# Three jobs taken from TensorE's transposes and fp32 products in a two-block hybrid layer

## The reference, cut to what matters

```python
# GDN (first layer): per head and chunk, from the log gates g
g_cum = cumsum(g); diff = g_cum[:, None] - g_cum[None, :]
decay = exp(where(incl, diff, 0)) * incl
# retention (second layer)
rq = rotary(rq.reshape(B, T, 8, 64), pos)
rk = rotary(rk.reshape(B, T, 8, 64), pos)
ret = chunk_retention(rq, rk, rv)         # products rk^T rq, weighted by distance
# cross attention (second layer): keys and values of the memory
kv = rmsnorm(mem, g_mem) @ w_xkv          # mem: (256, 1024)
```

## Time and profile before

| | us |
|---|---|
| median of 3 runs | 889.11 (888.86 to 889.22) |
| the profiled execution, its own time | 889.3 |
| its span | 887.5 |
| busy in the span: TensorE / VectorE / ScalarE / GpSimd | 879.3 / 594.3 / 440.9 / 167.7 |

### The profile page before, as it was taken

The page is one execution under the profiler, slowest core; times in us unless marked ns, Lnnn a source line. Parts: engine busy times, 40 slices in busy tenths (PEclk is TensorE's granted clock), DMA queues, the critical chain, the costliest instruction groups (busy, mean ns, idle before and its releaser), DMA issues.

```text
span 887.5 us, 12630 instructions
## 1 busy us (share of the span) xinstructions
PE 879.3 (99%) x4991; PEld 757.1 (85%) x4991; DVE 594.3 (67%) x868; ACT 440.9 (50%) x619; POOL 167.7 (19%) x181
## 2 busy tenths in 40 slices
PE   8999999999999999999999999999999999999998
PEld 6887887888988999988888889888888888889786
DVE  5478988996796666744456647977785576665542
ACT  6265456864545555533344436646555444443531
POOL 0432225765110000000000002100100024444700
PEclk9999999999999999999999999999999999999999
DMA  8874542344244666656577635523542567775762
GB/s 301 199 253 144 189 143 92 120 134 127 86 127 159 190 190 189 190 189 190 190 227 270 190 97 191 184 102 106 179 143 75 166 198 220 220 220 158 238 224 71
DMA packets 86627, 152.64 MB, mean 172 GB/s; under 512 B 10016, under 2 KB 18000, under 8 KB 86448
## 3 DMA queue, kind: packets, MB, share of 16 engines
q1 hardware_dynamic: 80352, 144.55, 50.8%
q0 software_dynamic: 3696, 3.76, 2.1%
q10 hardware_dynamic: 2528, 3.63, 1.1%
HBM read 147.59 MB, written 1.44 MB: 168 GB/s over the span
## 4 chain that ended last, share of the span: by engine, by line
PE 95%; DMA 3%; ACT 1%; POOL 1%; DVE 0%; issue 0%; SPq 0%
PE gemm L515 71%; PE gemm L1012 5%; PE mixbank L1012 5%; DMA raw<-in_w_in_dram 2%; PE mixbank L578 2%; PE mixbank L677 1%; PE mixbank L702 1%; DMA raw<-in_w_down_dram 1%; PE mixbank L782 1%; PE mixbank L873 1%; PE mixbank L1184 1%; PE gemm L1212 1%; PE mixbank L688 1%; PE mixbank L725 1%; POOL w_lo L2647 1%; PE mixbank L1101 0%
## 5 line engine op out<-in xcount | busy, mean ns | idle before, releaser
L1825 DVE TENSOR_TENSOR w_lo<-raw,w_hi 128x2048 fp32r<-128x2048 f32 (+3 forms) x131 | 285.3, 2187 | 181.5 <-ACT w_hi L1274 181.4
L1274 ACT ACTIVATE w_hi<-raw 128x2048 fp32r<-128x2048 f32 (+3 forms) x140 | 255.5, 1833 | 196.9 <-DMA raw<-in_w_in_dram 48.8
L515 PE MATMUL gemm<-w_hi,s_hi 128*128 128x512 f32 (+3 forms) x784 | 208.7, 386 | 0.5 <-ACT s_hi L1298 0.3
L515 PE MATMUL gemm<-w_lo,s_hi 128*128 128x512 f32 (+3 forms) x784 | 201.7, 377 | 0.1
L515 PE MATMUL gemm<-w_hi,s_lo 128*128 128x512 f32 (+3 forms) x784 | 201.7, 377 | 0.0
L515 PEld LDWEIGHTS gemm<-w_lo,s_hi 128*128 128x128 f32 x784 | 142.6, 188 | 27.7 <-DVE w_lo L1825 0.3
L515 PEld LDWEIGHTS gemm<-w_hi,s_lo 128*128 128x128 f32 x784 | 142.7, 188 | 27.6
L515 PEld LDWEIGHTS gemm<-w_hi,s_hi 128*128 128x128 f32 x784 | 139.8, 188 | 26.5 <-issue 2.5
L2653 POOL TENSOR_TENSOR sm<-sm 128x2 f32<-128x2 f32 (+5 forms) x13 | 21.6, 1662 | 453.1 <-DVE sm L1869 297.3
L2778 POOL DMA_DIRECT2D hid_moved<-hid_blocks x96 | 54.9, 580 | 70.0 <-DVE hid_blocks L2596 67.8
L2647 POOL TENSOR_TENSOR w_lo<-raw,w_hi 128x2048 fp32r<-128x2048 f32 x9 | 41.4, 4609 | 39.1 <-ACT w_hi L1274 39.1
(11 more groups left out here) (353 smaller groups left out, 1172.3 us busy)
## 6 DMA issues: line engine op xcount, KB each, us to landing
raw<-in_w_in_dram SPq DMA_DIRECT2D x40, 1024.0 KB, 5.1
raw<-in_w_mlp_up_dram SPq DMA_DIRECT2D x16, 1024.0 KB, 5.6
raw<-in_w_mlp_down_dram SPq DMA_DIRECT2D x16, 1024.0 KB, 5.1
raw<-in_w_gate_dram SPq DMA_DIRECT2D x10, 1024.0 KB, 5.4
raw<-in_w_up_dram SPq DMA_DIRECT2D x10, 1024.0 KB, 5.1
raw<-in_w_down_dram SPq DMA_DIRECT2D x10, 1024.0 KB, 5.4
raw<-in_w_out_dram SPq DMA_DIRECT2D x8, 1024.0 KB, 5.1
raw<-in_w_xkv_dram SPq DMA_DIRECT2D x8, 1024.0 KB, 5.1
```

The lines of the kernel that those rows point to most:

```text
L515: return nc.tensor.matmul(G[b % 2][t][:, 0:width], lhs, rhs, start=kt == 0 and not (low_x or low_w), stop=kt == blk["kt"] - 1 and (low_x i ...
L1274: nc.scalar.activation(w_hi[:, n % SLOTS, 0:kn, 0:width], raw[:, n % SLOTS, 0:kn, 0:width], ACT.Copy)\
L1825: V.tensor_tensor(w_lo[:, s, 0:kn, 0:width], raw[:, s, 0:kn, 0:width], w_hi[:, s, 0:kn, 0:width].bitcast(F32), ALU.subtract)\
```

## The change

**Memory rows.** They are loaded earlier (after `squares(1)`), into the space beside the first MLP's hidden values. At the first block of that MLP's down projection VectorE turns their 32x32 squares (`turn_squares`, four instructions of 128x512). When `B_2` may begin, GpSimd issues 16 DMAs of 64 KB (`move`) that put the squares in place. `memory_hi` and `memory_lo` split from SBUF, the first half of them before the retention output is evacuated, the second behind it. The 16 transposes of line 578 are gone. `squares(3)` moves to the start of `B_2`, behind `squares(2)`.

**Retention.** After the rotation VectorE turns the squares of queries and keys (four of 128x512), GpSimd issues 16 DMAs of 64 KB, and the products of line 1079 read the moved tile. The 16 transposes of line 1066 and the four copies are gone.

**Decay rows.** The gates are split in `gates_hi` and `gates_lo` (three small instructions and a copy of the triangular constant to fp32r on VectorE), GpSimd makes eight products of 128x512 in place of two of 128x1024, the first four of them already after `att_max` 2, and TensorE adds two fp32r matmuls per piece in place of one fp32 matmul.

**One chunk.** `w_lo` of chunk 1 of `B_D2` is made by VectorE between `up_mul(5)` and the split of chunk 2.

```diff
+        def move(eng, dst, src, name):
+            d, s = (v.rearrange("p (n j b) -> p n j b", j=4, b=32) for v in (dst, src))
+            for i in range(4):
+                for j in range(4):
+                    eng.dma_start(d[32 * j:32 * j + 32, :, i, :], s[32 * i:32 * i + 32, :, j, :]).then_inc(sem(name), 16)
...
-        BY_POOL = {...} | {(B_D2, 1)}
+        BY_POOL = {...}
...
             def decay_rows(u):
-                nc.tensor.matmul(DECAYS[u % 2][:, :], cst[:, C_AFTER:C_AFTER + P], src, start=True, stop=True).then_inc(sem("gdn_bc"), 1)
+                nc.tensor.matmul(DECAYS[u % 2][:, :], after_r[:, :], hi, start=True, stop=False)
+                nc.tensor.matmul(DECAYS[u % 2][:, :], after_r[:, :], lo, start=False, stop=True).then_inc(sem("gdn_bc"), 1)
...
-            pe.wait_ge(sem("ret_rot"), 1)
-            for e in range(4): ... nc.tensor.transpose(...)      # 16 of them
             mm(B_2 + 4)
             mm(B_2 + 5)
-            pe.wait_ge(sem("ret_act"), 2)
-            pe.wait_ge(sem("ret_dve"), 2)
+            pe.wait_ge(sem("ret_moved"), 16 * 16)
...
-            pe.wait_ge(sem("mem_in"), 16)
-            turn(lambda kt, t: MEM[:, t, P * kt:P * kt + P], ...)
             mm(B_KV, turned=20)
...
# ScalarE
             squares(1, x)
+            act.dma_start(mem_rows[:, :, :], mem_2[0].rearrange("(t p) d -> p t d", p=P)).then_inc(sem("mem_in"), 16)
...
             squares(2, x)
+            act.wait_ge(sem("mem_in"), 16)
+            squares(3, mem_rows)
...
+            memory_hi(range(2))
             for t in range(NT):
                 act.wait_ge(sem("ret_o"), t + 1)
                 nc.scalar.activation(MG2[:, t, 0:NCOL], M[2 + t][:, :], ACT.Copy).then_inc(sem("ret_oc"), 1)
-            turn_hi(NORMS["mem"])
+            memory_hi(range(2, 4))
             begin(B_KV)
-            squares(3, MEM)
...
# VectorE
+            V.tensor_copy(after_r[:, :], cst[:, C_AFTER:C_AFTER + P])
...
+            link(V.tensor_copy(gates_hi[:, :], GA_))
+            V.tensor_tensor(gates_lo[:, :], GA_, gates_hi[:, :].bitcast(F32), ALU.subtract).then_inc(sem("gdn_g"), 1)
...
+                if j == 0:                                       # first block of B_DN
+                    dve.wait_ge(sem("mem_in"), 16)
+                    turn_squares(mem_blocks, mem_rows).then_inc(sem("mem_blocks"), 1)
...
-                    sig(rotate(...), "ret_rot")
+                    link(rotate(...))
+                    dve.wait_ge(sem("stat_ss"), 8)
+                    turn_squares(RET_BLOCKS, P2R).then_inc(sem("ret_blocks"), 1)
...
+            memory_lo(range(2))
             ...                                                  # sums of the retention output
-            turn_lo(NORMS["mem"])
+            memory_lo(range(2, 4))
...
-            begin(B_GU + 11)
+            split(B_D2, 0)
             up_mul(5)
+            split(B_D2, 1)
             split(B_D2, 2)
# GpSimd
-            pool.wait_ge(sem("att_norm"), 6)
-            for t in range(NT): pool.tensor_tensor(GU[...], ...)
+            pool.wait_ge(sem("att_max"), 2)
+            for u in range(4):
+                if u == 2:
+                    pool.wait_ge(sem("att_norm"), 6)
+                for part, dst in ((gates_hi, GU_HI[u]), (gates_lo, GU_LO[u])): ins = pool.tensor_tensor(dst, ...)
+                ins.then_inc(sem("gdn_gu"), 1)
...
             norm_power(2)
+            pool.wait_ge(sem("mem_blocks"), 1)
+            for t in range(NT):
+                pool.wait_ge(sem(f"ev{t}"), B_2)
+            move(pool, MEM, mem_blocks[:, :], "mem_moved")
+            pool.wait_ge(sem("ret_blocks"), 1)
+            move(pool, RET_MOVED, RET_BLOCKS, "ret_moved")
             power("fox", RNF, SSF, 32)
```

More of the change, by code:

```diff
@@ L195, in build @@
         a1.close()
+        a5 = ExitStack()
+        gu_hi = sb("gu_hi", [P, 16, P], F32R, a5)
+        sb("below_gu_lo0", [P, 19632 - 16 * P], F32, a5)
+        gu_lo0 = sb("gu_lo0", [P, 4, P], F32R, a5)
+        sb("below_gu_lo23", [P, 4, P], F32, a5)
+        gu_lo23 = sb("gu_lo23", [P, 8, P], F32R, a5)
+        sb("below_gu_lo1", [P, 2, P], F32, a5)
+        gu_lo1 = sb("gu_lo1", [P, 4, P], F32R, a5)
+        a5.close()
+        GU_HI = [gu_hi[:, 4 * u:4 * u + 4, :] for u in range(4)]
+        GU_LO = [gu_lo0[:, :, :], gu_lo1[:, :, :], gu_lo23[:, 0:4, :], gu_lo23[:, 4:8, :]]
         a2 = ExitStack()
@@ L797, in _ @@
             turned_in(2)
-            pe.wait_ge(sem("gdn_gu"), 1)
-            decay_rows(0)
-            decay_rows(1)
+            for u in range(2):
+                pe.wait_ge(sem("gdn_gu"), u + 1)
+                decay_rows(u)
             fill(1)
@@ L1059, in _ @@
                 mm(B_2 + j, turned=None if j else 16)
-            pe.wait_ge(sem("ret_rot"), 1)
[L1062 to L1067, removed]
             mm(B_2 + 4)
             mm(B_2 + 5)
-            pe.wait_ge(sem("ret_act"), 2)
-            pe.wait_ge(sem("ret_dve"), 2)
+            pe.wait_ge(sem("ret_moved"), 16 * 16)
+            rows = RET_MOVED.rearrange("p (t k n) -> p t k n", t=NT, n=P)
+            rq, rk = rows[:, :, 0:4], rows[:, :, 4:8]
             for half in range(2):
@@ L1078, in _ @@
                         q = 2 * half + j
-                        last = nc.tensor.matmul(M[2 * par + half][:, 256 * j:256 * j + 256], rkT[64 * par:64 * par + 64, q, 0:P],
-                                                rqT[64 * par:64 * par + 64, q, :], start=True, stop=True)
+                        o = M[2 * par + half][:, 256 * j:256 * j + 256].rearrange("p (t n) -> p t n", n=P)
+                        last = nc.tensor.matmul(o, rk[64 * par:64 * par + 64, 0, q], rq[64 * par:64 * par + 64, :, q], start=True, stop=True)
                         if j == 1:
@@ L1118, in _ @@
             pe.wait_ge(sem("fox_aug"), 1)
+            pe.wait_ge(sem("ret_oc"), 2)
             for e in range(8):
@@ L1291, in project, with memory_hi, turned_by_pe @@
                 nc.scalar.activation(dst, G[b % 2][0][:, 0:blocks[b]["n"]], ACT.Copy, scale=scale).then_inc(sem("ev0"), 1)
+            def memory_hi(pairs):
+                for q in pairs:
+                    act.wait_ge(sem("mem_moved"), 16 * 16)
+                    for kt in (2 * q, 2 * q + 1):
+                        ins = nc.scalar.activation(token_tile(s_hi[:, kt, :]), moved(MEM, kt), ACT.Copy, scale=gains[:, NORMS["mem"], kt:kt + 1])
+                    sig(ins, "turn_hi")
+            def turned_by_pe():
+                return seen.get("turn_hi", 0) + 1 - (KT // 2 if seen.get("turn_hi", 0) >= 20 else 0)
             def turn_hi(norm=None, banks=range(4)):
                 for q in banks:
-                    act.wait_ge(sem("turn_pe"), seen.get("turn_hi", 0) + 1)
+                    act.wait_ge(sem("turn_pe"), turned_by_pe())
                     if norm is None:
@@ L1864, in turn_lo, with memory_lo, turn_squares @@
                     sig(ins, "turn_lo")
+            def memory_lo(pairs):
+                for q in pairs:
+                    dve.wait_ge(sem("turn_hi"), seen["turn_lo"] + 1)
+                    for kt in (2 * q, 2 * q + 1):
+                        ins = V.scalar_tensor_tensor(token_tile(s_lo[:, kt, :]), moved(MEM, kt), gains[:, NORMS["mem"], kt:kt + 1],
+                                                     token_tile(s_hi[:, kt, :]).bitcast(F32), ALU.mult, ALU.subtract)
+                    sig(ins, "turn_lo")
+            def turn_squares(dst, src):
+                for t in range(NT):
+                    for half in range(2):
+                        cols = slice(NCOL * half, NCOL * half + NCOL)
+                        ins = V.transpose(dst[:, D * t:D * t + D][:, cols], src[:, t, cols])
+                return ins
             def mean_squares(norm):
```

64 lines of the change are left out of this document (29 added, 35 removed).

## The result

The changed kernel takes 893.66 us (891.97 to 893.84, 5 runs) where the kernel before takes 889.22 beside it: ratio 1.0042, interval 1.003 to 1.0053. It is 4.4 us slower; the forecast was 5.4 us faster, and the range ended at 886.3. The profiled execution has its own time at 893.7 us, span 891.9, against 889.3 and 887.5.

What follows compares the result with a forecast made beforehand. TensorE was taken as the bound, busy 879.3 of 887.5 us. 1.76 + 1.67 + 1.46 + 0.92 - 0.4 = 5.4 us off the 889.1 median gave 883.7 us, range 882.8 to 886.3.

Steps and rivals of the forecast that it cites:

- Gains: TensorE time saved: retention transposes 1.76 us, memory transposes 1.67, decay rows 1.46, one chunk's wait 0.92.
- The turning at `B_2 + 3`: VectorE's retention turning delays `w_lo`: 0.3 us wait plus 0.10 restart, 0.4 charged, ends 0 and 1.0.
- as for the weights: Moves beside weight loads from `B_2` on: 3.5 us of all 16 DMA engines per move, priced at nothing, end 0.5.
- (a): Rival: VectorE or ScalarE late at several tight places at once, 1.8 us more, 885.5, up to 886.5; chance 0.16.
- my marks: Trace signs: new TensorE wait on VectorE's `w_lo`, 0.1 to 0.5 us near 492; wrong if busy falls under 4.5.
- Gate copies: First attention: VectorE gets some 0.6 us more, 0.46 of it in an existing wait; cost 0 to 0.2, taken 0.
- (b): Rival: the decay rows run at the price of before, 1.46 us less gain, 885.2; chance 0.04.
- (c): Rival: GpSimd held whenever VectorE works, 64 KB DMAs cost double, TensorE waits 18.4 us, 902; chance 0.04.
- Retention moves landing in time: Retention DMAs landed by 509 (518 by the bound), wanted at 526.4: hidden with at least 8 us to spare.
- the forget gates without a wait: TensorE at the forget gates: 0.5 of 0.9 us slack remains, so no wait; end 0.5 us.

Runs made afterwards that it cites:

- paced: Changed kernel with both moves issued in four groups of four DMAs, one behind each weight chunk TensorE has done; 884.18 us, ratio 0.9948.
- paced_all: Changed kernel with both moves in groups of four, retention squares turned behind both `w_lo` of `B_2 + 3`, gate copies late, retention table at `B_2 + 4`; 883.89 us.
- table_late: Changed kernel with the 1.5 MB retention table loaded behind the third block instead of at `B_2`; 891.06 us, ratio 1.0017.
- moves_only: Kernel before plus 16 unneeded DMAs of the memory move's shape, issued by GpSimd when `B_2` begins; 895.92 us, ratio 1.007.
- paced_mem: Changed kernel with only the memory move in groups of four DMAs, the retention DMAs still back to back; 884.91 us, ratio 0.9947.
- moves_paced: Kernel before plus 16 unneeded DMAs of the memory move's shape, four behind each weight chunk TensorE has done; 889.83 us, ratio 1.0009.
- mem_long: Changed kernel with the memory move's same bytes in 2 KB pieces instead of 128-byte ones, memory keys and values not the reference's; 890.45 us, ratio 1.0015.
- turn_after: Changed kernel with both `w_lo` of `B_2 + 3` made ahead of the turning of the retention squares; 890.43 us, ratio 1.0009.
- moves_no_table: Kernel before plus 16 unneeded DMAs of the memory move's shape all at once, retention table loaded at `B_2 + 4`; 891.11 us, ratio 1.0025.
- mem_late: Changed kernel with the 16 retention DMAs issued first and the 16 memory DMAs behind them; 889.64 us, ratio 1.0004.

## Why the prediction was wrong

- **Gains: right.** 1.76, 1.67, 1.46 and 0.92 were forecast. The stage differences read 1.69, 1.55 and 1.08 for the last three. In paced the stage of the first, retention, gains 1.49 with the 0.26 of the next point still in it, so 1.75 without. The runs that hold one edit alone gave 1.45 (decay, copies late) and 0.9 (chunk), each clear of none but no finer than about 0.8 us either way. With every loss mended, paced_all is 5.4 under before by the medians, which is the gain that was forecast for the kernel as it stood.
- **The turning at `B_2 + 3`: right with weights on time.** 0.4 forecast. In paced TensorE waits there 1.05 - 0.91 = 0.14, and the group behind costs 1.03, 0.12 more: 0.26.
- **The failed step** is "as for the weights ... Nothing, with an end of 0.5 us". It put the price of the moves for the weight loads at nothing, and the runs show a stall of 6.60 us behind those loads. Two things were wrong in it. The size: 56 engine-us per MB came from DMAs of 32 KB in another stretch; the memory move, in the same 128-byte pieces, took 120 for its 1.05 MB. In paced it took 13.1% of 20 us x 16 = 42 for 0.52 MB, 80 per MB, so this time is no constant of the move. And the test: I set an average share of 0.59 over 62 us beside a move spread over it. The move is issued in 10.4 us, and at the very start of the 62, where the table comes in as well. Before, that window had 0.79 x 20 x 16 = 253 engine-us, with the memory rows in them, which the changed kernel loads earlier. At q10's 40 per MB (32.0%, 2.54 MB) those are some 42, so 211 stay. With the measured 120 that makes 331 of the 320 that there are. With the 59 of my own price it would have made 270, a share of 0.84: much tighter than 0.59, a reason to look for the late load, but not yet the loss. It took both mistakes.
- **What that set off.** Chunks 4.8 and 7.2 us late cost nothing by themselves; TensorE had buffered work. They pushed VectorE's list, with 6.9 us of rotation and 2.5 of turning in it, past the next `w_lo`. No rival had this chain: (a) had 0.5 us for the weight loads and no link from them to VectorE. The slower clock was 2.55 us on top. Two of my marks were missed with it: a new wait on VectorE's `w_lo` was to show 0.1 to 0.5 us near 492, and it shows 6.60 us before 501.69; the busy time of TensorE was to fall by 4.5 us or more, and it fell by 1.7.
- **Gate copies: costed at 0 to 0.2, cost 0.5.** I checked ScalarE's exponentials behind them and not the `w_lo` that was next in VectorE's own queue, and took a 0.46 us wait for slack of that `w_lo`. It belongs to the following one.
- **(b) and (c) fell**, by the decay rows and by the 651 ns issues. Retention moves landing in time, and the forget gates without a wait: right.

How the loads were stretched has a rule beside it. In the traces, weight chunks land after 5.4 us with the table and the memory rows beside them (before), 8.2 with the move alone (table_late), 12.3 with the move and the table (the changed kernel), 14.6 with all three (moves_only). The Trainium skill, page "DMA: Bandwidth & Descriptors", section "🔬 Queues, rings and completion order", says that each DMA engine takes turns, packet by packet, between the queues that have work for it; by that rule a burst in one queue takes its share from the weights' queue however urgent they are, and the trace agrees in direction. The Trainium skill, page "DMA: Bandwidth & Descriptors", section "Why small descriptors are slow (HBM only)", says that transfers within SBUF don't suffer from small pieces. Here the rows differ: 120 engine-us in 128-byte pieces, 68 in 2 KB ones, in the same window. The measurement decides for this window; a fixed price of the small pieces it does not give, since they took 56 per MB in the last MLP and 80 in paced.

What stays open: why retention's burst costs 0.7 us by the medians (paced_mem against paced, not clear of noise) where memory's cost 6 to 9. The table is not the reason: the burst of table_late has none beside it and still costs 4.8 us of waiting. Nor is the DMA share, 0.95 at 484 to 500 in paced_mem. One difference fits the chain above: behind memory's late chunk stand the rotation and the turning in VectorE's list, 9.4 us, and behind retention's, which is 4.8 us late too, comes the `w_lo` at once. No run tests that.

## What to carry to other kernels

A transfer off the path is judged by the stretch in which it is issued, not by the stretch in which it has to be done: add its engine time to the DMA share of just those microseconds, and when that comes near 1.0 ask which load will be late and who is behind it on every in-order queue. The share alone does not tell: from 464 to 484 moves_paced has 1.00 and no wait follows, table_late has 0.92 and 4.8 us follow. What parts the runs is when the late load arrives: ScalarE starts `w_hi` of the second chunk of `B_2 + 2` at 477.1 to 479.8 in before, paced and moves_paced, where TensorE does not wait, and at 481.5 to 485.0 in mem_long, table_late, turn_after, the changed kernel and moves_no_table, where it does. If the move has time to spare, spread it and start it later: one wait per four DMAs did both and was worth 9.5 us here, by the medians. Test a suspected order or placement again after the main fault is mended; its worth changes (3.2 us before, none after).

## What the runs showed of the hardware that I had not expected

- A stall costs more than itself. Waits of 2.55, 3.47, 4.75 and 6.60 us (mem_late, turn_after, table_late, the changed kernel) were followed by groups of 1.4 to 1.9 us in place of 0.91, in sum 1.4 to 2.6 us more; in the changed kernel the granted clock in that stretch was 0.52. The sum does not simply follow the wait: 4.29 us in mem_long cost 2.6, 4.75 in table_late 1.5. Waits of 0.2 to 0.8 us cost some 0.1.
- Beside the weights and the table, 128-byte pieces within SBUF took 1.75 times the engine time of 2 KB pieces (120 against 68 engine-us for 1.05 MB). The same small pieces took 80 per MB when they were paced: the bytes and the size of the pieces alone do not fix the engine time of a transfer.
- One megabyte moved in a burst beside the weights, the table and the memory rows cost the kernel before 6.6 us, the same megabyte in four groups from 7 us later on 0.6.
